# A two-layer hybrid decoder trunk in split float32: the first merged piece is turned by the DMA instead of TensorE, and the steps around it are put in another order

## What is computed

```python
x = x + 0.5 * swiglu_ffn(rmsnorm(x, norm_ffn1[l]), w_ffn1_in[l], w_ffn1_out[l])
u = rmsnorm(x, norm_mix[l])
q, k, v, g, p, c, gates = jnp.split(u @ w_in[l], split_points, axis=-1)
y_ret = (retention(q, k, v, positions) * jax.nn.silu(g)) @ w_ret_out[l]
y_pool = pool_mixer(p, w_pool[l], pool_scale[l])
y_conv = conv_module(c, conv_w[l], conv_b[l], conv_ln_g[l], conv_ln_b[l], w_conv_out[l])
gates = jax.nn.sigmoid(gates + gate_bias[l]).reshape(B, S, N_BRANCHES, D)
merged = gates[:, :, 0] * y_ret + gates[:, :, 1] * y_pool + gates[:, :, 2] * y_conv
x = x + merged @ w_out[l]
x = x + 0.5 * swiglu_ffn(rmsnorm(x, norm_ffn2[l]), w_ffn2_in[l], w_ffn2_out[l])
```

## Time and profile before

| | us |
|---|---|
| median of 3 runs | 1128.8 |
| lowest and highest | 1128.4, 1129.02 |
| the profiled execution | 1129.01 |
| its span in the profile | 1127.2 |

### The profile page before, as it was taken

One profiled execution on the slowest core, in us unless ns is written; L12 is line 12 of the kernel. 1 busy time (PEld: TensorE's weight loads), 2 busy tenths in 40 slices (PEclk: granted clock), 3 DMA queues, 4 the chain that ended last, 5 costly groups with the idle time before them and its releaser, 6 DMA issues.

```text
span 1127.2 us, 13064 instructions
## 1 busy us (share of the span) xinstructions
PE 1119.7 (99%) x5006; PEld 926.0 (82%) x5006; DVE 802.6 (71%) x985; ACT 649.8 (58%) x744; POOL 30.3 (3%) x68
## 2 busy tenths in 40 slices
PE   9999999999999999999999999999999999999997
PEld 7888888888888888888888888888888878888886
DVE  6856565899999775655476655478999987665553
ACT  7755535763657675554475554376637476756442
POOL 0000000000100000000000000000000001000000
PEclk9999999999999999999999999999999999999999
DMA  9976666763756787666497666478638677866551
GB/s 357 333 249 208 219 238 192 248 210 116 252 217 196 205 289 219 210 201 226 143 299 252 205 206 230 165 223 244 192 121 274 231 191 218 276 220 224 159 187 38
DMA packets 130862, 244.65 MB, mean 217 GB/s; under 512 B 99040, under 2 KB 100448, under 8 KB 106224
## 3 DMA queue, kind: packets, MB, share of 16 engines
q1 hardware_dynamic: 128016, 236.61, 64.2%
q0 software_dynamic: 1648, 6.06, 1.5%
q10 hardware_dynamic: 1136, 1.15, 0.3%
HBM read 219.16 MB, written 1.05 MB: 195 GB/s over the span
## 4 chain that ended last, share of the span: by engine, by line
PE 94%; DMA 2%; DVE 1%; SPq 1%; ACT 1%; issue 0%; POOLq 0%; POOL 0%; DVEq 0%; ACTq 0%
PE acc L419 31%; PE acc L420 31%; PE acc L421 31%; DMA raw<-in_weights 1%; DMA retT_planes<-ret_planes 1%; SPq L754 1%; DVE w_lo L1248 1%; ACT w_hi L817 0%; PE tr L604 0%; PE tr L595 0%; SPq L395 0%; PE tr L513 0%; DVE gates L1556 0%; PE ret L614 0%; PE ret L618 0%
## 5 line engine op out<-in xcount | busy, mean ns | idle before, releaser
L1248 DVE TENSOR_TENSOR w_lo<-raw,w_hi 128x2048 fp32r<-128x2048 f32 (+2 forms) x204 | 445.0, 2211 | 86.0 <-ACT w_hi L817 86.0
L817 ACT CAST w_hi<-raw 128x2048 fp32r<-128x2048 f32 (+2 forms) x204 | 375.0, 1849 | 212.3 <-PE acc L421 205.3
L419 PE MATMUL acc<-w_hi,xT_hi 128*128 128x512 f32 x1152 | 451.1, 392 | 0.5 <-DVE w_lo L1248 0.5
L421 PE MATMUL acc<-w_hi,xT_lo 128*128 128x512 f32 x1152 | 448.5, 389 | 0.0
L420 PE MATMUL acc<-w_lo,xT_hi 128*128 128x512 f32 x1152 | 448.3, 389 | 0.0
L419 PEld LDWEIGHTS acc<-w_hi,xT_hi 128*128 128x128 f32 x1152 | 216.4, 188 | 46.3 <-DVE w_lo L1248 1.3
L421 PEld LDWEIGHTS acc<-w_hi,xT_lo 128*128 128x128 f32 x1152 | 216.3, 188 | 45.1
L420 PEld LDWEIGHTS acc<-w_lo,xT_hi 128*128 128x128 f32 x1152 | 216.4, 188 | 43.9
L1331 DVE SCALAR_TENSOR_TENSOR h<-acc,rs,silu_gate 128x256 f32<-128x256 f32 x88 | 42.4, 482 | 149.5 <-ACT silu_gate L884 149.5
L419 PE MATMUL acc<-w_hi,hT_hi 128*128 128x512 f32 x348 | 135.4, 389 | 0.0
L420 PE MATMUL acc<-w_lo,hT_hi 128*128 128x512 f32 x348 | 135.4, 389 | 0.0
(11 more groups left out here) (144 smaller groups left out, 648.8 us busy)
## 6 DMA issues: line engine op xcount, KB each, us to landing
raw<-in_weights SPq DMA_DIRECT2D x192, 1024.0 KB, 5.1
raw<-in_weights SPq DMA_DIRECT2D x20, 256.0 KB, 5.9
raw<-in_weights SPq DMA_DIRECT2D x8, 512.0 KB, 3.5
bias<-in_gate_bias POOLq DMA_DIRECT2D x6, 512.0 KB, 5.3
x<-in_x SPq DMA_DIRECT2D x2, 512.0 KB, 9.4
scale_row<-in_pool_scale POOLq DMA_DIRECT2D x2, 512.0 KB, 6.2
hT_planes<-h_planes SPq DMA_TRANSPOSE x54, 3.1
band<-in_band POOLq DMA_DIRECT2D x1, 768.0 KB, 6.5
```

The lines of the kernel that those rows point to most:

```text
L419: nc.tensor.matmul(o, a_hi, b_hi, start=first, stop=False)
L421: return nc.tensor.matmul(o, a_lo, b_hi, start=False, stop=last)
L817: nc.scalar.copy(w_hi[:, hf % HIGHS, 0:n], raw[:, hf % RAWS, 0:n]).then_inc(hi_split, 1)
L1248: nc.vector.tensor_tensor(w_lo[:, hf % RAWS, 0:n], raw[:, hf % RAWS, 0:n], w_hi[:, hf % HIGHS, 0:n].bitcast(F32), ALU.subtract).then_inc(l ...
```

## The change

The diff has four parts. PE no longer turns piece (0, 0): it is split, turned by the DMA and joined as the other three, with its high and low parts made in two instructions of two feature blocks each, and a new semaphore `merged_front` lets PE begin w_out after the first of them. The order of the steps on DVE and ACT from M_CONV to the seam is another. The first two additions into x and the first two splits of x move from the seam to between the steps of the pieces (1, 0) and (1, 1). At the start of the program x's second tile is loaded one weight half later, and ACT casts that half before it squares the tile.

```diff
         def moved(l, t, c):
-            return 3 * l + 2 * t + c - 1
+            return 4 * l + 2 * t + c
@@ PE
-            def turn_merged(l):
-                pe.wait_ge(merged_all, l * 4 + 1)
-                transpose4(("m", l), [merged[:, 0, 0, i * P:(i + 1) * P] for i in range(4)])
...
-                wide(l, M_CONV, M_CONV, 1, side, range(4), True, True,
-                     {(0, 1): lambda: turn_merged(l)})
-                wait_tr_taken(pe, ("m", l))
-                wide(l, M_OUT, M_OUT, 0, xT, range(4), True, False)
+                wide(l, M_CONV, M_CONV, 1, side, range(4), True, True)
+                pe.wait_ge(merged_front, l + 1)
+                wide(l, M_OUT, M_OUT, 0, xT, range(4), True, False,
+                     {(0, 1): lambda: pe.wait_ge(merged_lo_ready, moved(l, 0, 0) + 1)})
@@ SP
-                if t == c == 1:
-                    sp.wait_ge(merged_joined, moved(l, 0, 1) + 1)
+                if t == 1:
+                    sp.wait_ge(merged_joined, moved(l, 0, c) + 1)
...
-                if hf == FIRST + 1:
+                if hf == FIRST + 2:
                     load_x(1)
...
                 if hf % HALVES == 2 * FFN2:
+                    turn_merged(hf // HALVES, 0, 0)
                     turn_merged(hf // HALVES, 0, 1)
                     turn_merged(hf // HALVES, 1, 0)
-                if hf % HALVES == 2 * FFN2 + 1:
+                if hf % HALVES == 2 * FFN2 + 2:
                     turn_merged(hf // HALVES, 1, 1)
@@ ACT, seam and start
-                split_x(l, norm, 0, 0)
-                split_x(l, norm, 0, 1)
+                if norm != 3:
+                    split_x(l, norm, 0, 0)
+                    split_x(l, norm, 0, 1)
...
                     silu(l, f, 0, 0)
+                    cast(ahead(0) + 1)
                     square(l, 0, 1)
-                    cast(ahead(0) + 1)
@@ ACT, split_merged and merged_high
-                if t == c == 1:
-                    act.wait_ge(merged_turned[1], 16 * (2 * l + 1))
+                if t == 1:
+                    act.wait_ge(merged_turned[c], 16 * (2 * l + 1))
...
+                act.wait_ge(merged_joined, moved(l, t, c) + 1)
+                m = mT_whole[:, c, :].rearrange("p (k n) -> p k n", k=4)
+                n = 2 if t == c == 0 else 4
+                for i in range(0, 4, n):
+                    nc.scalar.activation(xT_hi[:, 4 * c + i:4 * c + i + n, tokens(t)],
+                                         m[:, i:i + n, :], ACT.Copy, scale=0.5
+                                         ).then_inc(x_hi_ready, 1)
@@ ACT, mixer
                 gate_tanh(l, CONV, 1, 1)
+                split_merged(l, 0, 0)
                 cast(ahead(M_CONV))
+                split_merged(l, 0, 1)
                 merged_high(l, 0, 0)
-                split_merged(l, 0, 1)
                 split_merged(l, 1, 0)
                 cast(ahead(M_CONV) + 1)
                 merged_high(l, 0, 1)
+                cast(ahead(M_OUT))
                 split_merged(l, 1, 1)
-                cast(ahead(M_OUT))
                 merged_high(l, 1, 0)
+                split_x(l, 3, 0, 0)
                 merged_high(l, 1, 1)
+                split_x(l, 3, 0, 1)
@@ DVE, seam
-                add_next(l, norm, 0, 0)
-                add_next(l, norm, 0, 1)
-                if own:
+                if norm == 3:
                     sub(hf)
+                else:
+                    add_next(l, norm, 0, 0)
+                    add_next(l, norm, 0, 1)
@@ DVE, mixer
+                merge(l, CONV, 0, 0, merged_all)
                 gate_z(l, CONV, 1, 1)
-                merge(l, CONV, 0, 0, merged_all)
                 sub(l * HALVES + 2 * M_CONV + 3)
                 merge(l, CONV, 0, 1, merged_all)
+                merged_join(l, 0, 0)
                 merged_low(l, 0, 0)
                 merge(l, CONV, 1, 0, merged_all)
+                merged_join(l, 0, 1)
                 sub(l * HALVES + 2 * M_CONV + 4)
-                merged_join(l, 0, 1)
-                merge(l, CONV, 1, 1, merged_all)
                 merged_low(l, 0, 1)
 
                 sub(l * HALVES + 2 * M_OUT + 3)
                 merged_join(l, 1, 0)
+                merge(l, CONV, 1, 1, merged_all)
+                merged_low(l, 1, 0)
+                add_next(l, 3, 0, 0)
+                add_next(l, 3, 0, 1)
                 merged_join(l, 1, 1)
-                merged_low(l, 1, 0)
                 merged_low(l, 1, 1)
 
-                seam(l, 3, l * HALVES + 2 * M_OUT + 4, True)
+                seam(l, 3, l * HALVES + 2 * M_OUT + 4)
```

36 lines of the change are left out of this document (15 added, 21 removed).

## The result

| | us |
|---|---|
| kernel before, median of 6 runs (lowest, highest) | 1129.11 (1128.4, 1130.07) |
| changed kernel, median of 6 runs (lowest, highest) | 1135.49 (1134.82, 1136.29) |
| ratio, with its 95% interval | 1.0056 (1.0045 to 1.0066) |
| the changed kernel's profiled execution, and its span | 1136.27, 1134.5 |

The forecast was 1135.3 with a range of 1131.9 to 1138.5, so the time and the sign were right. The two large terms were nearly right too: +3.8 and +3.0 were said, +3.8 and +2.6 are measured, though 0.4 of the measured 3.8 comes from a slow transpose that the sum did not hold. A term of 1 us in the mixer of layer 1 was not foreseen at all, and one sentence of the reasoning, that the moved additions buy nothing, turned out wrong by 3 us a layer.

The account below looks back on a forecast made before the run. PE, busy 99% of the span, was taken to bound the kernel through its matmuls and waits. Layer 0 +3.8, layer 1 +3.0 and the start -0.3 gave +6.5 us: 1128.8 becomes 1135.3, range 1131.9 to 1138.5.

Parts of the forecast that it names:

- The two large terms: Delay of x's last low part between conv and the FFN: +3.8 us in layer 0, +3.0 us in layer 1.
- the moved additions buy nothing: Before the seam: x's earlier additions gain nothing, since x's first join stands behind the last merged piece.
- The shift passes through whole: From x's first join to its last low part: the same instruction row in both kernels, so layer 0's 3.8 us carries through.
- The first piece's way: Piece (0, 0) from merge through split, DMA and join to w_out's first matmul: PE waits 0.65 us.
- The two half-size instructions: First piece's high and low parts for two blocks each: taken as 0.48 us apiece, lower bounds 0.32 and 0.34.
- What is queued behind it: Steps behind the first join: PE 0.7 us late at the second chunk's second half, split of (1, 1) 7.1 us later.
- Layer 1: The same walk from conv to x's first join in layer 1: a shift of 2.95 us, counted as +3.0.
- The start: Program start: x's second tile loaded later lets the sixth half's cast come earlier, gaining 0.3 us, possibly nothing.
- The rule that was weighed: Turning a piece: skill prefers TensorE for 128 x 128; PE takes 0.52 us against 3.0 us of DMA transit.
- Steps that overlap to half the shift: Rival: first piece's chain and fourth merge cost about half, shift 1.5 to 2 us a layer, 1132; chance 0.16.
- Waits hidden: Rival: the chain has slack, PE's waits stay under the turning's gain, all 2.0 us won, 1126.8; chance 0.08.
- Slow transposes: Rival: transposes sharing queues with weight loads; each like the 4.6 us one adds 1.5, two give 1138.5; chance 0.17.

Follow-up runs that it names:

- merge ahead of the join: The changed kernel with DVE's merge of the third piece (1, 0) put ahead of the first piece's join and low part: 1133.15 us.
- the free orders: Two kernels with newly chosen step orders between conv and the seam: DMA turns all four pieces, 1129.31 us; PE still turns the first piece, 1129.53 us.
- DMA turns, free order: The changed kernel reordered: first split ahead of the last gate, second merge ahead of the first join, last turn issued between the weight loads: 1129.31 us.
- the run with the late turn: The kernel before with piece (0, 0) turned by DMA, the start changed, and the last piece's turn issued behind both weight loads: 1138.13 us.
- the run with the additions in the seam: The changed kernel with x's two first additions and their splits put back in the seam, behind all four pieces' joins and low parts: 1141.0 us.

## Why the prediction was right, step by step

**What bounds the kernel, and how the shift is passed on.** Right in what bounds it: PE is at 99% again, and its losses are the waits. x's last low part starts at 399.52 where it started at 395.84; with conv 0.13 earlier that is 3.81, and the matmul behind it is 3.82 later. "The shift passes through whole" holds in layer 1 (2.56 at x's first join, 2.55 at the last matmul) and not in layer 0. There the first join is 3.43 later and not 3.8, and the missing 0.4 comes in at the end, where DVE waits 0.48 for x's last transpose. That the 3.8 was met all the same is luck: in both layers the shift walked for x's first join was 0.4 too large.

**The first piece's way.** Right within 0.4 us throughout: split at 355.75 (355.82 walked), SP at 356.80 (356.90), join at 359.86 (359.95), PE at 361.58 (361.8). The two half-size instructions, for which the trace before had no row, took 0.72 for two on ACT and 0.76 on DVE, so 0.36 and 0.38 apiece where 0.48 was assumed: near the lower bound (0.32 and 0.34), not near the 128 x 256 rows of other kinds that I chose. That term was too large by about 0.1 on each engine. The transposes took 3.0, the lower bound, eight of eight.

**What is queued behind it.** Right: split of (1, 1) 21.5 us after conv's first matmul (21.7 said), x's first join 29.9 (30.1 said). The wait for `w_lo` at the second half was said as 0.7 and is 0.71, in both layers. The runs confirm the ranking as well: w_out's first wait may grow and the time still falls (merge ahead of the join), while the new order, in which the last merge is late, carries 5.1 us even where PE turns the first piece.

**Layer 1.** +3.0 said, 2.56 and 2.69 measured. The term is 0.3 to 0.4 too large. In the first trace x's first join was 0.22 earlier than walked (29.85 after conv's first matmul, 30.07 said), for which the half-size instructions and the transposes at 3.0 go that way; the other 0.17 was added because the walk of the kernel before had come out early, while that of the changed kernel came out late. The same two parts make the 0.4 of layer 0.

**The start.** -0.3 said. The first matmul with x was 0.16 later than before in the trace and conv's first 0.13 earlier, so 0.29 was gained between them, as said, and the gap at 30 us is gone. In medians it can't be told from nothing.

**"The moved additions buy nothing."** Wrong, the step that failed. The walk compared x's join with the end of the last merged piece and stopped there: it took for granted that x's transpose would be there whenever the join's turn came. Put back, the additions start at 377.75, their transpose lands 1.5 us after DVE is ready for it, and each piece of x behind is late as well: 3.2 us more in layer 0 and 2.9 in layer 1. The sum didn't suffer, since it followed the changed order as it stands.

**The mixer of layer 1.** Missing from the sum: +1.0 in both traces. Term by term the first trace gives 0.16 - 0.29 + 3.81 + 1.02 + 2.56 = 7.26 where the sum had 6.5. The median came within 0.2 us of the forecast partly by luck: the walked shift was 0.4 too large in each layer, the slow transpose and the mixer gave that back and more, and the median moved by 6.4, less than the profiled execution did.

**The rule that was weighed.** The Trainium skill (VectorE: DVE Perf Modes, Rules for kernel authors) would have the turning on TensorE; in the changed kernel's order the runs agree by 1.0 us (1135.49 against 1134.46), though in the traces 0.8 of that lies in the mixer's stretch; in the free orders they show no difference (1129.31 and 1129.53). Its figures (Advanced Engine Details and Errata, X-Bar Transpose; DMA: Bandwidth & Descriptors) had led to 2.7 us a transpose; the trace shows 3.0 for all eight, so the rows were the better end.

**The rivals.** Steps that overlap to half the shift: no, the layer is 3.8. Waits hidden: no in this order, though an order exists in which they are (DMA turns, free order). Slow transposes: not the merged pieces' in the changed kernel, but the rival's mechanism is real and larger than it was priced. A turn behind two weight loads took 6.6 us, more than the 4.6 that was the worst row before, and its place in the queue cost 5.8 us in all. One of x's transposes did slow the changed kernel in layer 0, by 0.4.

## What to carry to other kernels

In this kernel a piece's turn by DMA cost no time that can be measured once its data was made early and it was issued early (1129.31 against 1129.41); what it costs is decided by where its split, its merge and its issue stand in four in-order queues, so walk each candidate order up to the last consumer before the code is moved. Issue a short transpose ahead of the big loads and not behind them, which was worth 5.8 us here. And price a moved step only together with the order around it: the same two additions saved 5 us in one order and cost 2 in another, depending on whether their engine would otherwise have waited for the DMA or had to wait for PE.

## What the runs showed of the hardware

- Transit of a 256 KB transpose, from issue to landing: 3.0 us when the queue is free, 6.6 and 7.1 behind two 1 MB weight loads, up to 9.3 among the mixer's loads. x's last piece in layer 0, also issued among loads, took 6.0 or 6.1 in three traces and 7.3 to 8.1 in the eleven others, with nothing between.
- PE's granted clock after a wait. In the run with the late turn a gap of 2.24 us between two matmuls (373.13 to 375.37) was followed by some eight matmuls at up to 0.43 us, the 1.2 GHz level. In the run with the additions in the seam a gap of 2.17 us (388.75 to 390.92) was followed by matmuls at 0.23 us, and the window behind it has the full clock:

```profile
390.90:395.10 4.20, 4.18 (x18) 1.00 0.78 140
```

  So two waits of the same length, one with a loss of 1.5 us behind it (2.68 long in layer 1, the same loss) and one with none in either layer. No gap of up to 1.6 us at full clock was followed by slower matmuls in any of the traces. Shorter gaps lay close ahead of both: 0.93 and 0.94 us within 8 us of the first, 1.41 us within 5 us of the second. What tells the two apart was not tried.
